# Projection steps between the attention heads, the norm folded into the router, and a fused scale, mask and row maximum

## What is computed

```
x = rmsnorm(x, g_final)                      # end of the first block
z = rms_norm(x, norm1_g) @ w_in              # q, k, v (8 heads of 64) and a conv input
q, k = rope(rms_norm(q, k per head))
attn: three dilated windows, mixed by their log-sum-exps
conv: 31-tap depthwise conv, layer norm, silu
x = x + concat(attn, conv) @ w_out
h = rms_norm(x, norm2_g)
aff = softmax(h @ w_router)                  # 256 x 16 experts
each expert takes its 32 best positions:
x[idx] += gate * ((silu(xt @ w1) * (xt @ w3)) @ w2)      # w1, w3: 1024 x 2816, w2: 2816 x 1024
```

## Time and profile before

| | |
|---|---|
| median of 3 runs | 1923.91 us (1923.51 to 1924.23) |
| the profiled execution | 1921.09 us |
| its span in the trace | 1919.2 us |
| TensorE busy | 1380.4 us (72%) |
| VectorE busy | 283.3 us (15%) |
| ScalarE busy | 214.1 us (11%) |
| GpSimd busy | 35.1 us (2%) |
| moved by DMA | 648.95 MB, mean 338 GB/s |

### The profile page before, as it was taken

How to read it: one execution, slowest core, us unless ns; L and a number is a source line. 1 busy time by engine, 2 the same in 40 slices (tenths; PEclk the granted TensorE clock), 3 DMA queues, 4 the chain that set the end, 5 groups by cost and what they waited for, 6 DMA issues and landing times.

```text
span 1919.2 us, 23551 instructions
## 1 busy us (share of the span) xinstructions
PE 1380.4 (72%) x10490; PEld 846.8 (44%) x10490; DVE 283.3 (15%) x551; ACT 214.1 (11%) x417; POOL 35.1 (2%) x59
## 2 busy tenths in 40 slices
PE   5997899999978765656656666665665666666565
PEld 3674788888746532323323233232332323323232
DVE  1115200004972310100101001010010100101001
ACT  2222222002133200000000000000000000000000
POOL 0000000001010000000000000000000000000000
PEclk8998899999989787777777777777777777778778
DMA  9458224334232499999999999999999999999998
GB/s 353 164 203 344 112 106 175 132 132 152 81 128 121 181 433 434 424 431 440 433 424 436 427 441 424 436 435 424 433 436 435 432 424 437 434 433 425 430 439 342
DMA packets 47523, 648.95 MB, mean 338 GB/s; under 512 B 3752, under 2 KB 6256, under 8 KB 30976
## 3 DMA queue, kind: packets, MB, share of 16 engines
q1 hardware_dynamic: 44432, 643.90, 79.5%
q10 hardware_dynamic: 2848, 3.54, 0.5%
q0 software_dynamic: 208, 1.00, 0.1%
HBM read 647.37 MB, written 1.06 MB: 338 GB/s over the span
## 4 chain that ended last, share of the span: by engine, by line
DMA 57%; PE 11%; DVE 1%; ACT 1%; issue 1%; SPq 0%; DVEq 0%; ACTq 0%; PEldq 0%
DMA ring<-in_w 57%; PE ps L1085 11%; PE ps L1433 0%; ACT arena L634 0%; PE ps L1095 0%; DVE small L983 0%; DVE arena L981 0%; ACT arena L622 0%; ACT arena L478 0%; DVE small L984 0%; DVE arena L835 0%; DVE arena L1036 0%; DVE arena L1002 0%; DVE arena L1038 0%; DVE arena L990 0%
## 5 line engine op out<-in xcount | busy, mean ns | idle before, releaser
L1085 PE MATMUL ps<-ring,arena 128*32 128x352 f32 (+2 forms) x6914 | 637.4, 533 | 448.3 <-DMA ring<-in_w 439.2
L1085 PEld LDWEIGHTS ps<-ring,arena 128*32 128x32 f32 (+1 forms) x6914 | 259.4, 134 | 823.7 <-issue 494.9
L1085 PE MATMUL ps<-arena 128*128 (+9 forms) x972 | 197.3, 396 | 28.4 <-DVE arena L1077 12.2
L1085 PE MATMUL ps<-hT,ring 128*128 128x256 f32 (+1 forms) x912 | 198.8, 380 | 7.2 <-ACT hT L566 3.5
L1085 PEld LDWEIGHTS ps<-arena 128*128 128x128 f32 (+6 forms) x972 | 161.2, 255 | 66.9 <-issue 40.0
L1085 PEld LDWEIGHTS ps<-hT,ring 128*128 128x128 f32 (+1 forms) x912 | 171.1, 188 | 35.0 <-issue 8.2
L1085 PE MATMUL ps<-arena,ring 128*128 128x256 f32 x768 | 171.0, 384 | 2.4 <-ACT arena L572 1.2
L1085 PEld LDWEIGHTS ps<-arena,ring 128*128 128x128 f32 x768 | 147.7, 193 | 24.1 <-issue 2.6
L1077 DVE TENSOR_TENSOR arena<-arena,ps 128x512 f32<-128x512 f32 x64 | 41.7, 685 | 336.9 <-PE ps L1085 336.8
L678 ACT ACTIVATE arena<-ps 128x256 f32<-128x256 f32 x16 | 6.1, 384 | 726.6 <-PEq L1537 726.6
L1066 DVE TENSOR_TENSOR arena<-arena,ps 128x704 f32<-128x704 f32 x16 | 14.2, 888 | 457.8 <-ACT arena L676 457.8
(11 more groups left out here) (200 smaller groups left out, 482.4 us busy)
## 6 DMA issues: line engine op xcount, KB each, us to landing
ring<-in_w SPq DMA_DIRECT2D x80, 5632.0 KB, 32.9
ring<-in_w SPq DMA_DIRECT2D x16, 2816.0 KB, 28.6
ring<-in_w SPq DMA_DIRECT2D x32, 1408.0 KB, 32.0
ring<-in_w_ff SPq DMA_DIRECT2D x8, 4096.0 KB, 13.3
ring<-in_w_ada SPq DMA_DIRECT2D x6, 4096.0 KB, 13.8
ring<-in_w_in SPq DMA_DIRECT2D x4, 4096.0 KB, 17.8
ring<-in_w_in SPq DMA_DIRECT2D x3, 2048.0 KB, 10.7
ring<-in_w_out SPq DMA_DIRECT2D x1, 4096.0 KB, 14.2
```

The source lines that it names most:

```text
L1085: return pe.matmul(o, w, x, start=first, stop=last)
```

## The change

1. Units wo2_0 and wo2_1 become one unit wo2. SyncE loads expert 0's slots 9 to 11 once qk is used, 0 to 5 as before once v is used, and 6 to 8 once wo2 is used; the first refill of four slots becomes slots 12, 13, and 14 with 15, each waiting for the chunks that it needs.
2. v1 is made in three parts: four chunks before cm, three after rt, one after the first two tc. ScalarE's copy of it moves behind the conv's root.
3. A head's scale, mask and maximum are one tensor_tensor_reduce per 128 queries; the mask table holds the logarithms of the counts times 8, or -1e30. ScalarE's exp sums the rows itself. VectorE writes a diagonal matrix of the inverse sums, and TensorE multiplies by it where it transposed.
4. The projection runs by input chunk: 64 products in 8 steps into four held banks zb0 to zb3, which start with xT (GpSimd has multiplied it by g_final before). Conv chunks 4 to 7 come at i = 4 to 7, attention chunks 0 and 1 at i = 8, 2 and 3 at the end. VectorE copies the banks to xT.
5. The router multiplies xT by w_router times norm2_g, with a 17th row for the sum of squares; the root and reciprocal are taken on 128x2 after turning, and go into the exp as its scale. hnat comes from xT, scaled per position, and norm2_g is put on in the copies of the expert input, by chunk.
6. Top-8 reads PSUM, its results are kept side by side, and one scan goes. pick is written for expert 0 first.
7. In the expert loop two chunks are gathered ahead, each further one behind a w1 chunk, alternating banks 7 and 3; pgs is turned after w1.

```diff
@@ SyncE
-            for i, (q, n) in enumerate(PIECE_AT):
-                if q < NSLOT:
-                    sp.wait_ge(s["unit_used"], block_free(q + n - 1))
-                    if q < 3:
-                        sp.wait_ge(s["qf_set"], 4)
-                        sp.wait_ge(s["conv_set"], TAPS * CT)
-                        sp.wait_ge(s["xr_set"], 1)
-                else:
-                    sp.wait_ge(s["w_used"], q + n - NSLOT)
-                piece(0, i)
+            sp.wait_ge(s["unit_used"], UNIT["qk"] + 1)
+            slots(0, 9, 3, s["first_in"])
+            sp.wait_ge(s["unit_used"], UNIT["v"] + 1)
+            sp.wait_ge(s["qf_set"], 4)
+            sp.wait_ge(s["conv_set"], TAPS * CT)
+            sp.wait_ge(s["xr_set"], 1)
+            piece(0, 0)
+            slots(0, 4, 2, s["first_in"])
+            sp.wait_ge(s["unit_used"], UNIT["wo2"] + 1)
+            slots(0, 6, 2, piece_in[1])
+            slots(0, 8, 1, piece_in[2])
+            for q, n, done in ((12, 1, s["refill_in"]), (13, 1, s["refill_in"]), (14, 2, piece_in[3])):
+                sp.wait_ge(s["w_used"], q + n - NSLOT)
+                slots(0, q, n, done)
@@ GpSimd
+            pool.dma_start(iota, T["table3"]).then_inc(s["consts2_in"], 16)
-            nc.gpsimd.tensor_scalar(neg2, cnt2, 0.0, NEG, ALU.is_equal, ALU.mult).then_inc(s["neg_set"], 1)
+            nc.gpsimd.tensor_tensor(wr2[:, :, 0:NE], wr.rearrange("p (c e) -> p c e", c=C),
+                                    g2.unsqueeze(2).broadcast_to([P, C, NE]), ALU.mult).then_inc(s["wr2_set"], 1)
             nc.gpsimd.tensor_tensor(xT, xT, r1.unsqueeze(1).broadcast_to([P, C, S]), ALU.mult).then_inc(s["xr_set"], 1)
+            pool.wait_ge(s["xr_set"], 1)
+            nc.gpsimd.tensor_tensor(xT, xT, g_final.unsqueeze(2).broadcast_to([P, C, S]), ALU.mult).then_inc(s["xr_set"], 1)
-            nc.gpsimd.tensor_tensor(conv, conv, csq, ALU.mult).then_inc(s["mixc_set"], 1)
+            for m in (0, 2):
+                nc.gpsimd.tensor_tensor(mix2[:, 4 + m:6 + m, :], mix2[:, 4 + m:6 + m, :], csq[:, m:m + 2, :], ALU.mult)\
+                    .then_inc(s["mixc_set"], 1)
@@ ScalarE
-            take("v1", vn[:, 1, :], bk("v1"), s["v_set"], 2)
...
+            take("v1", vn[:, 1, :], bk("v1"), s["v_set"], 2)
+            for i in range(MH + 1):
...
-                        A(sl, sl, ACT.Exp, bias=mneg[:, 2 * (i % 2) + st:2 * (i % 2) + st + 1])\
+                        A(sl, sl, ACT.Exp, bias=mneg[:, 2 * b + st:2 * b + st + 1],
+                          accum_out=rsum[:, 2 * b + st:2 * b + st + 1]).then_inc(s["texp_set"], 1)
-                        A(sl, sl, ACT.Copy, scale=rinv[:, 2 * (j % 2) + st:2 * (j % 2) + st + 1])\
-                            .then_inc(s["tp_set"], 1)
-                if i == 5:
+                if i == 3:
                     act.wait_ge(s["cln_set"], CT)
                     A(flat(csq), flat(mix2[:, 4:8, :]), ACT.Sigmoid).then_inc(s["csg_set"], 1)
...
-                act.wait_ge(s["xe_full"], e + 1)
-                A(flat(xe), ps[:, 7, 0:S], ACT.Copy).then_inc(s["xe_set"], 1)
+                for c in range(C):
+                    act.wait_ge(s["xe_full"], C * e + c + 1)
+                    A(xe[:, c, :], ps[:, (7, 3)[c % 2], c * CAP:(c + 1) * CAP], ACT.Copy, scale=g2rows[:, c:c + 1])\
+                        .then_inc(s["xe_set"], 1)
@@ VectorE
-                    link(V.scalar_tensor_tensor(buf, bk(f"tc{i}"), HD ** -0.5, neg2, ALU.mult, ALU.add))
+                    for st in range(ST):
+                        half = slice(st * S, (st + 1) * S)
+                        ins = V.tensor_tensor_reduce(buf[:, half], bk(f"tc{i}")[:, half], lnc[:, half], HD ** -0.5,
+                                                     2 * NEG, ALU.add, ALU.max, mx[:, st:st + 1])
+                    link(ins)
                     empty(dve, f"tc{i}")
-                    link(V.reduce_max(mx, buf.rearrange("p (st k) -> p st k", st=ST), AX.X))
...
-                        ins = V.scalar_tensor_tensor(sl, sl, 1.0, cnt2[:, st * S:(st + 1) * S], ALU.mult, ALU.mult,
-                                                     accum_out=rsum[:, 2 * b + st:2 * b + st + 1])
+                    link(V.reciprocal(rinv[:, 2 * b:2 * b + 2], rsum[:, 2 * b:2 * b + 2]))
+                    for st in range(ST):
+                        V.tensor_scalar(diag[:, b, st * P:(st + 1) * P], ident[:, :], rinv[:, 2 * b + st:2 * b + st + 1],
+                                        None, ALU.mult).then_inc(s["diag_set"], 1)
...
-                if i == 1:
+                if i == 0:
                     dve.wait_ge(s["cvar_set"], 1)
                     V.reciprocal(lnr, lnr).then_inc(s["crec_set"], 1)
...
+            for k in range(4):
+                wait_filled(dve, f"zb{k}")
+                V.tensor_copy(xT_[:, 2 * k * S:(2 * k + 2) * S], bk(f"zb{k}")).then_inc(s["x2_set"], 1)
+                if k >= 1:
+                    pair_squares(k - 1)
...
-            link(V.tensor_copy(flat(place), bk("rk")[:, 0:ST * NE]))
-            empty(dve, "rk")
+            V.tensor_tensor(pick[:, :, 0:CAP], iota.unsqueeze(1).broadcast_to([P, ST, CAP]),
+                            place[:, :, 0:1].broadcast_to([P, ST, CAP]), ALU.is_equal).then_inc(s["pick_set"], 1)
             for st in range(ST):
-                ins = V.tensor_tensor(pick[:, st, :].rearrange("p (e t) -> p e t", e=NE),
+                ins = V.tensor_tensor(pick[:, st, CAP:].rearrange("p (e t) -> p e t", e=NE - 1),
...
             dve.wait_ge(s["rank_set"], 1)
+            empty(dve, "rk")
             dve.sem_inc(s["pick_set"], 1)
             dve.wait_ge(s["yinit_set"], 8)
 
             dve.sem_inc(s["he_set"], 1)
@@ TensorE
-            proj_rows("v1", w, 0, hT, 1, last=True)
+            wait_emptied(pe, "v1")
+            v1_part(0, 4)
             pe.wait_ge(s["conv_set"], TAPS * CT)
             wait_emptied(pe, "cm")
...
+            v1_part(4, 7)
             pe.wait_ge(s["csq_set"], 1)
             wait_emptied(pe, "cv")
...
+            def z_start(k):
+                wait_emptied(pe, f"zb{k}")
+                mm(bk(f"zb{k}"), ident[:, :], xT_[:, 2 * k * S:(2 * k + 2) * S], True, False)
+
+            def z_step(c, last=False):
+                for m in range(C):
+                    done = last and m % 2 == 1
+                    ins = mm(bk(f"zb{m // 2}")[:, (m % 2) * S:(m % 2 + 1) * S], wo2[:, c, m * P:(m + 1) * P],
+                             mix2[:, c, :], False, done)
...
+            def z_conv(c):
+                pe.wait_ge(s["mixc_set"], 1 + (c - 4) // 2)
+                z_step(c)
...
+                if i == 0:
+                    finish("v1", v1_part(7, 8))
+                if i == 1:
+                    pe.wait_ge(s["xr_set"], 2)
+                if i in (1, 2):
+                    z_start(2 * i - 2)
+                    z_start(2 * i - 1)
+                if 4 <= i <= 7:
+                    z_conv(i)
                 if 1 <= i <= MH:
                     j = i - 1
                     b = j % 2
-                    pe.wait_ge(s["tp_set"], 2 * j + 2)
                     wait_emptied(pe, f"uT{j}")
-                    for kt in range(ST):
-                        for st in range(ST):
-                            ins = pe.transpose(bk(f"uT{j}")[:, kt * S + st * P:kt * S + (st + 1) * P],
-                                               tcb[j % 3][:, st * S + kt * P:st * S + (kt + 1) * P], ident[:, :])
+                    for st in range(ST):
+                        pe.wait_ge(s["diag_set"], 2 * j + st + 1)
+                        for kt in range(ST):
+                            ins = mm(bk(f"uT{j}")[:, kt * S + st * P:kt * S + (st + 1) * P],
+                                     tcb[j % 3][:, st * S + kt * P:st * S + (kt + 1) * P],
+                                     diag[:, b, st * P:(st + 1) * P], True, True)
                     inc_filled(ins, f"uT{j}")
+                if i == MH:
+                    z_heads(0)
+                    z_heads(1)
...
+            z_heads(2)
+            z_heads(3)
+
+            pe.wait_ge(s["wr2_set"], 3)
+            wait_emptied(pe, "lgT")
+            for k in range(5):
+                for c in (2 * k, 2 * k + 1):
+                    if c < C:
+                        pe.wait_ge(s["x2_set"], k + 1)
+                        mm(bk("lgT")[0:17, 0:S], wr2[:, c, :], xT[:, c, :], c == 0, False)
+                if k >= 1:
+                    pe.wait_ge(s["sqp_set"], k)
+                    ins = mm(bk("lgT")[0:17, 0:S], one16, sq2[:, 2 * k - 2, :], False, k == 4)
+            inc_filled(ins, "lgT")
...
-                pe.wait_ge(s["xe_set"], 1 + e)
-                for c in range(C):
+                def gather(c):
                     for st in range(ST):
-                        ins = mm(ps[:, 7, c * CAP:(c + 1) * CAP],
+                        ins = mm(ps[:, (7, 3)[c % 2], c * CAP:(c + 1) * CAP],
                                  hnat[:, st, c * P:(c + 1) * P],
```

(10 more changed lines are left out.)

284 lines of the change are left out of this document (157 added, 127 removed).

## The result

The changed kernel takes 1904.99 us (median of 4, 1901.62 to 1906.49) where the kernel before took 1923.9 beside it (median of 3; a fourth execution of 3402.72 us is left out): ratio 0.9903, interval 0.9886 to 0.992. Forecast were 1903.1 and a range of 1895 to 1911. The profiled execution took 1906.49 us, its span is 1904.3.

The account below looks back on a forecast made before the run. The prediction took the expert weight stream as the bound: first refill plus 1255 us. Terms -0.2 - 5.6 - 6.8 - 9.7 + 1.5 = -20.8 us give span 1898.4, plus 4.7 to the median: 1903.1 us, range 1895 to 1911.

Parts of the forecast that it names:

- What bounds it: Whole kernel: expert weight stream at 80.1 us per expert; time is the moment of the first refill plus 1255 us.
- Convolution to first head: Stage up to the first head: blocked taps +2.8, v1 split -3.5, TensorE's work +0.4; -0.2 us in all.
- The block: Convolution taps: GpSimd's g_final product blocks VectorE for 4.5 us, less 1.7 of reserve, +2.8 us.
- Rival 1: Convolution: GpSimd does not block the taps, heads start 2.8 us earlier, 1900 us; chance 0.17.
- Heads and projection: First head to last z: TensorE nearly full, 58.2 us of work plus waits, 65.5 instead of 71.1, -5.6 us.
- Both waits: Heads: TensorE waits 2.2 us before the first uT and 2.8 before z step 4.
- the turned probabilities: Heads: 64 real product passes instead of 32 transposes on TensorE, 12.6 us.
- Router: Last z to first gather: shorter way to top-8 -6.1, picks -0.3, split +0.3, start -0.7; -6.8 us together.
- First gather to first refill: Start of the expert loop: two gathers, one chunk at the low level, one-slot refill; 4.2 us instead of 13.9, -9.7.
- What the small refills lose: Weight stream after the first refill: a gap while gathers and chunks reach the fourth, +1.5 us (0 to 3).
- Rivals 2 and 4: Heads: TensorE's clock low for longer, 1908 to 1912 us, chance 0.17; low until the last z step, about 1960, 0.03.
- Afterwards nothing: Expert loop after the first refills: copies, gathers and pgs turn hide under TensorE's 439 us of weight waits, no cost.

Follow-up runs that it names:

- no g product: Changed kernel without GpSimd's product of xT by g_final (output lacks that factor, timing only): 1900.78 us, ratio 0.9894 to the kernel before.
- The corners: Changed kernel with diagonals or scaled copies, projection steps between heads or late; first tc to lgT: diagonals 63.0 and 60.5 us, scaled copies 58.9 and 67.3.
- One-slot refills: Changed kernel with expert 0's slots 12 to 19 refilled one at a time, each behind its own chunk: ratio 0.9875 to the kernel before.
- the repeat: The changed kernel timed again without any edit: 1903.64 us, ratio 0.9896 to the kernel before.
- gathers first: Changed kernel with all eight gathers of each expert ahead of w1, ScalarE's copies waiting for all of them: ratio 0.9888 to the kernel before.
- one head later: Changed kernel with the four projection steps of conv chunks 4 to 7 moved back by one head: ratio 0.9878 to the kernel before.
- the early signal: Changed kernel with VectorE's first he_set ahead of the two wide pick instructions instead of behind them: ratio 0.9894 to the kernel before.
- both, with the z steps late: Changed kernel with slots 12 to 19 refilled singly, first he_set before the wide picks, all projection steps behind the head loop: 1897.94 us, ratio 0.9869.
- z steps late: Changed kernel with six projection steps (conv chunks 4 to 7, head groups 0 and 1) moved behind the head loop: ratio 0.9896 to the kernel before.
- scaled copies, z late: Changed kernel with ScalarE scaling the probabilities, TensorE turning them with the identity, and all projection steps behind the head loop: ratio 0.993.

## Why the prediction was right, and where not

The forecast was 1.9 us below the median measured, and part of that nearness is luck. Counted from the reciprocal, the profiled execution gained 16.5 us where the sum said 20.8: the refills lost 7.7 us more than forecast, and heads and convolution gave 3.9 more. With 1.6 us lost upstream, its span came 5.9 us above the forecast (1904.3 against 1898.4). The median came only 1.9 above, since the prediction added 4.7 us from span to median where 0.7 were measured: the profile before was 2.8 us faster than its median, the one after 1.5 slower than its own.

*What bounds it.* Right: 80.1 us per expert before and after, and the time follows the first refill. The first refill came at 640.02 us (forecast near 643, though its own terms give 664.3 - 22.3 = 642.0), 24.1 earlier.

*Convolution to first head.* Forecast -0.2, measured -1.3 in the profile (-2.9 with the shorter of the two clock steps). The block is real, 3.3 us of taps where 4.5 were charged, as the product itself took 3.60 us, not L393's 4.51; "no g product" shows that the path pays 1.1 of it, against the runs with the same clock step. Rival 1 is refuted by the taps' row and by that run. By the rule of the Trainium skill, "SBUF — State Buffer", section "Who interferes with whom", a VectorE instruction with two SBUF inputs and a GpSimd instruction that reads SBUF exclude each other; the taps with and without the product, 8.99 and 5.69 us, agree with it.

*Heads and projection.* Forecast -5.6, measured -8.4 (71.1 to 62.7 at the last z bank). Both waits were at their places, 1.63 and 2.36 us (forecast 2.2 and 2.8); the turned probabilities took 8.7 us where 12.6 were added, and one stretch at the low clock took 1.7. The step's picture of a full TensorE was right. What it left out is which part pays: the sum treats diagonals and interleaving as one gain. The corners suggest, with one execution each, that either cures ScalarE's latency, that both together are no better, and that as placed they cost 4 us in front of step 4, which the sum had as a wait of 2.8 and not as something to be moved.

*Router.* Forecast -6.8, measured -6.5 (26.0 to 19.5). The first gather stood behind the wide picks, as said; freeing it gave 0.7 us.

*First gather to first refill.* Forecast 4.2 us, measured 4.5.

*What the small refills lose.* This term of the sum was mis-sized: forecast +1.5 with 0 to 3 as its bounds, measured +9.2 (1264.3 against 1255.1). It covered "gathers and chunks up to the fourth, about 5 us", with one chunk at the low level. The fourth chunk came 10.5 us behind the first refill and the next bundle asked for the eighth, at 22.8 us, as the clock stayed at 0.50 through all of w1. Charging all eight chunks 3.50 us, and holding each bundle's request against what DMA had left to do, would have found it: slot 13 is in at 3.50 + 3.34 = 6.8 us and the next request comes at 10.5, slots 14 and 15 are in at 17.2 and the next comes at 22.8, gaps of 3.7 and 5.6 us, 9.3 together. "One-slot refills" takes 5.7 of the repeat's 9.9 away and "gathers first" all of it at the price of a later start. Rivals 2 and 4 put the low clock in the heads; what cost was the one that began in the router's wait and lasted through the gathers.

*Afterwards nothing.* Right, though TensorE lost 67 us of its waiting for weights.

## What to carry to other kernels

When a stream is asked for in bundles by an engine's progress, the first bundles after an empty ring are priced by that engine's real pace there, clock included; ask slot by slot until the stream leads. Two cures for one latency, another engine's form and work to fill the wait, need not add up: build the four corners. Filler whose own input comes late is a new wait; one head later was worth 4 us of 63 here. Joining the steps one head later with the one-slot refills and the early signal was not run; from the rows it should give, over "both, with the z steps late", 1.6 us more where neither has the low stretch in the first heads (60.5 - 58.9), and up to 3.3 where one run has it (62.2 - 58.9), an estimate.

## What the runs showed of the hardware

- TensorE, busy 5.00 of 5 us in window after window, kept the 1.2 GHz level from the first gather at 635.5 to 662.0 us, while gathers (32 moving columns) alternated with the 352-column products. Once the gathers stood ahead of them it was back at 0.93 in the second window of w1. With the changed kernel's order of work there it rose 5 and 8 us behind the first gather in two of twelve profiled executions ("z steps late" and "scaled copies, z late"); what decides it is open. The end, counted from the first refill, is 7 to 8 us earlier then with bundled refills, 1257.6 and 1256.7 against 1265.0. A spread of this size in unprofiled executions (1892.52 to 1903.36 with the steps one head later, mean clock 0.807 in the lowest and 0.797 to 0.801 in the others) fits it but isn't shown to be it.
- A VectorE form of 128x2 elements, 0.17 us alone, took 1.74 us beside GpSimd's 2.35 us product in the first heads, on the path to the first uT.
- The fused multiply, add and maximum from PSUM and SBUF costs no more than a plain copy of its length, 0.42 us for 256 columns, and 0.08 us to read its result.
